# Weight splits, the last turn of the local attention and the latent queries put in another order

## Chip, core and metric

The kernel runs on one NeuronCore of a Trainium2 chip. The metric is the device time of one execution in microseconds, as the median of the runs taken. TensorE (PE) multiplies, VectorE (DVE), ScalarE (ACT) and GpSimd (POOL) work beside it, and SyncE (SP) issues most of the weight loads. The engines are programmed separately and meet only at semaphores, so each works through its own list in order, and whatever waits at the head of a list holds all that is queued behind it.

## What is computed

Three transformer layers run over 256 latent tokens of width 1024 (and 256 context tokens in the first). The first two are a block with modulated norms: layer 0 has a convolution beside a neighbourhood attention ("a0" in the kernel) and a SwiGLU, layer 1 has a window attention and a differential attention ("a1") and a mixture of eight experts. The third layer is this, cut to what matters:

```python
xn = rms_norm_2(h, norm_mix_pre)
proj = xn @ w_in
...
gates = jax.nn.sigmoid(proj[..., IN_A + IN_B:] + b_gate)
g_a, g_b = gates[..., :D_MODEL], gates[..., D_MODEL:]
o_a = mixer_dilated(qkv_a, pos) @ w_o_a
o_b = mixer_mla(q_c, kv_c, k_pe, pos, mla_q_norm, w_uq, mla_kv_norm, w_ukv) @ w_o_b
mix = (g_a * o_a + g_b * o_b) @ w_out
h = h + rms_norm_2(mix, norm_mix_post)
hn = rms_norm_2(h, norm_mlp_pre)
ff = jnp.square(jax.nn.relu(hn @ w_ff1)) @ w_ff2
h = h + rms_norm_2(ff, norm_mlp_post)
```

`mixer_dilated` is an attention of 12 heads in three groups of different stride, whose outputs are weighted by their log-denominators and summed ("a2" in the kernel). `mixer_mla` takes the latent queries to 8 heads of 96 columns, of which 32 are rotated, and the latent keys and values to 8 heads of 64 and 64, and attends over all 256 tokens ("a3").

## The kernel before

Every large product is made from three products at reduced precision. A value x is split in hi (a copy of x in the engine's reduced type, made on ACT) and lo (x minus hi, made on DVE), and `mm3` (lines 889 to 892) adds lo·hi, hi·lo and hi·hi. Weights are split in the same way after their load: a tile of up to 128x2048 lies in one of a few slots, `raw`, `whi` and `wlo`. SP loads it when the tile that used the slot before has been consumed, ACT makes `whi` (line 1468) and DVE makes `wlo` (line 1983).

When ACT and DVE make these splits is set by `feed`, called all over their programs. `feed(event)` makes every split that is due for the tiles in use at that event, and `at["ahead"]` tiles more, as far as their slots allow (`next_tiles`). With `ahead` 2 a split is made two tiles early, with 0 only tiles already in use are made. A split is a single long instruction in the engine's list: what is queued behind it waits for it, and for the load it needs.

PSUM is eight banks; `take(ring, ...)` hands them out in turn from a ring (8 is all banks, 4 is banks 0 to 3), and PE waits there until the holder before has been read out. `Due` and `did` keep the semaphore values, so a wait already implied is not written again.

The places around the change:

- Before attention a0 the keys of layer 0 are turned (`l0_turned`, `head_hi`): for each of four row tiles PE transposes, DVE scales the result into `XQ` (line 2325), ACT makes hi (line 1513) and DVE lo (line 2050). PE's first score of a0 waits for the last lo. The call `feed(("ht", "k", t))` stands ahead of this work, with `ahead` 2 for t = 3.
- A norm of two row tiles: ACT sums the squares (line 1474), DVE makes the mean (`means`, line 2055), POOL takes it to the power -0.5 (`rsqrt`, line 2982), then DVE scales the even tile (line 2062) and ACT the odd one (line 1479). PE transposes both (line 896). In `norm_turned` DVE and ACT read the transposes and split them for the product. `means` of the odd tile is DVE's last step ahead of `norm_turned`, whose first step is a `feed`.
- Attention a2 ends with `finished`: a chain of ten small DVE operations and one ACT exponential, then five of 128x256 (lines 2202 to 2212) that give the last rows, `YA[1]` (mix__281 in the profile). PE turns them (`fin`), ACT makes hi and DVE lo into `OAT`, which is needed only after a3, in the product with w_o_a.
- Then PE makes the latent queries (`uq`, two tiles), keys and values (`ukv`, two tiles). ACT applies the sigmoid to the gates (line 1891), copies the queries out scaled (line 1902), DVE copies keys and values out (lines 2867, 2870) and rotates the queries (`rotate`, lines 2780 to 2787). PE turns queries and keys (`mqt`, eight groups), ACT and DVE copy them out, and a3 starts with scores that need all of them.
- After the product with w_out, `post` adds its norm: two sums, the mean, the power on POOL, then the scaled addition to h; `norm_scale("t", ...)` follows for the next norm. A `feed` stands within `post_scaled`.

In `post` the order on DVE is this (lines 2917 to 2929):

```python
means("pms", (name, t), m, D, ("v", at["chain"]))
post_scaled(name, 1, t, bk, yo, gn)
for half in range(2):
    hs = slice(half * 512, half * 512 + 512)
    for s, n in due(("prs", name, t), ("pyo", name, half, t)):
        e.wait_ge(s, n)
    e.scalar_tensor_tensor(out=h_t[t][:, hs], in0=yo[:, hs], scalar=m, in1=h_t[t][:, hs], op0=ALU.mult,
                           op1=ALU.add).then_inc(*did("post", name, t, half))
```

`("prs", name, t)` is POOL's power, which waits for `means`; `post_scaled` is the `feed` and then bank times gain.

## Time and profile before

| | us |
|---|---|
| median of 3 runs | 1921.24 (1919.27 to 1925.32) |
| the profiled execution | 1925.34, span 1923.5 |
| PE busy in the span | 1751.9 (91%) |
| DVE busy | 1250.8 (65%) |
| ACT busy | 824.2 (43%) |
| POOL busy | 134.6 (7%) |
| mean granted clock of PE | 0.943 |

All times of the trace are microseconds from the span's start. A row of the timeline has the start, the duration, the engine, the line, the operation, the tiles out<-in with their shapes, a count where instructions are merged, and in brackets the idle time before it with what ended it. Where rows of one engine overlap a little, the next instruction had begun while the one before was draining; so the step from start to start is what an instruction costs in a row of them. Names: `ps` is any PSUM bank, `keep__58` the small tile of sums, means and maxima, `in__75` the keys' hi of layer 0, `mix__264` and `mlp__289` the odd row tile of a norm, `mix__242` the latent queries, `whi__66`/`wlo__65` the two parts of a weight tile.

### The profile page before, as it was taken

What the parts mean: (1) busy time and instruction counts of PE and PEld (TensorE: products, weight loads), DVE (VectorE), ACT (ScalarE), POOL (GpSimd) and SP (SyncE); (2) the same over time, 40 slices, a digit from 0 to 9 for tenths busy, and PEclk for the clock granted to TensorE, in tenths of its full rate; (3) what the DMA queues carried; (4) which work ended last, traced back from release to release, by engine and by line L of the source; (5) the groups of instructions that cost most, each with busy time, mean ns of one, the idle gap of its engine ahead of it and who ended that gap; (6) DMA issues with size and microseconds to landing.
All of it is one profiled execution on the core that took longest, in us unless ns stands there. A gap on an engine that the chain in (4) does not pass through costs nothing. (4 is left out here: it accounts for less than half of the span.)

```text
span 1923.5 us, 22047 instructions
## 1 busy us (share of the span) xinstructions
PE 1751.9 (91%) x8958; PEld 1466.7 (76%) x8958; DVE 1250.8 (65%) x1709; ACT 824.2 (43%) x999; POOL 134.6 (7%) x128
## 2 busy tenths in 40 slices
PE   4896999899999987899979999999969998889998
PEld 2774777788788866798768888888859766669986
DVE  5356686368755544675668888888886554566643
ACT  5322232422212213333356667776744434435532
POOL 1130000200110011320100000000120000000000
PEclk9896999999999998899869999999999989999999
DMA  7431332245655431211148898888854511144553
GB/s 294 112 110 66 132 132 89 86 175 218 237 212 180 149 137 66 88 45 56 63 162 300 320 336 328 316 321 317 323 202 159 200 60 39 66 149 171 190 187 126
DMA packets 61437, 332.59 MB, mean 173 GB/s; under 512 B 16836, under 2 KB 17411, under 8 KB 28178
## 3 DMA queue, kind: packets, MB, share of 16 engines
q1 hardware_dynamic: 56080, 321.54, 46.4%
q10 hardware_dynamic: 4354, 6.32, 1.0%
q0 software_dynamic: 896, 3.26, 0.5%
q8 instruction: 74, 1.21, 0.3%
q14 instruction: 33, 0.26, 0.0%
HBM read 329.96 MB, written 1.13 MB: 172 GB/s over the span
## 5 line engine op out<-in xcount | busy, mean ns | idle before, releaser
L1983 DVE TENSOR_TENSOR wlo__65<-raw__64,whi__66 128x2048 fp32r<-128x2048 f32 (+2 forms) x64 | 149.4, 2335 | 95.6 <-ACT whi__66 L1468 95.6
L1983 DVE TENSOR_TENSOR wlo__61<-raw__60,whi__62 128x2048 fp32r<-128x2048 f32 (+2 forms) x65 | 145.1, 2232 | 94.3 <-ACT whi__62 L1468 94.2
L1468 ACT ACTIVATE whi__62<-raw__60 128x2048 fp32r<-128x2048 f32 (+2 forms) x65 | 118.9, 1829 | 115.3 <-DMA raw__60<-in_ffn_w 62.7
L1468 ACT ACTIVATE whi__66<-raw__64 128x2048 fp32r<-128x2048 f32 (+2 forms) x64 | 120.7, 1886 | 102.7 <-DMA raw__64<-in_ffn_w 37.9
L1983 DVE TENSOR_TENSOR wlo__69<-raw__68,whi__70 128x2048 fp32r<-128x2048 f32 (+4 forms) x50 | 106.6, 2133 | 28.3 <-ACT whi__70 L1468 28.2
L2016 DVE SCALAR_TENSOR_TENSOR wsum__71<-raw__68,silu_rows 128x1024 f32<-128x1024 f32 x84 | 100.0, 1220 | 5.4 <-DMA raw__68<-in_ada_w 4.9
L1468 ACT ACTIVATE whi__70<-raw__68 128x2048 fp32r<-128x2048 f32 (+4 forms) x50 | 87.5, 1750 | 13.7 <-DMA raw__68<-in_w_ff 11.6
L2982 POOL TENSOR_TENSOR keep__58<-keep__58,keep__59 128x1 f32<-128x1 f32 (+3 forms) x48 | 49.2, 1027 | 630.9 <-DVE keep__58 L2055 630.9
L2238 DVE TENSOR_REDUCE keep__58<-ps 128x1 f32<-128x256 f32 (+1 forms) x104 | 56.6, 545 | 23.2 <-PE ps L892 16.4
L1983 DVE TENSOR_TENSOR wlo__229<-raw__228,whi__230 128x2048 fp32r<-128x2048 f32 (+1 forms) x24 | 50.7, 2111 | 11.7 <-ACT whi__230 L1468 11.7
L1983 DVE TENSOR_TENSOR wlo__225<-raw__224,whi__226 128x2048 fp32r<-128x2048 f32 (+1 forms) x24 | 52.8, 2200 | 0.0
L890 PE MATMUL ps<-ffn__120,wlo__61 128*128 128x512 f32 (+1 forms) x128 | 46.9, 367 | 4.6 <-DVE ffn__121 L2050 3.3
L1468 ACT ACTIVATE whi__226<-raw__224 128x2048 fp32r<-128x2048 f32 (+1 forms) x24 | 42.5, 1771 | 11.4 <-DMA raw__224<-in_moe_w 11.4
L892 PE MATMUL ps<-ffn__120,whi__62 128*128 128x512 f32 (+1 forms) x128 | 46.4, 362 | 0.0
L891 PE MATMUL ps<-ffn__121,whi__62 128*128 128x512 f32 (+1 forms) x128 | 46.4, 362 | 0.0
L890 PE MATMUL ps<-ffn__120,wlo__132 128*128 128x512 f32 x112 | 43.7, 390 | 0.9 <-issue 0.9
L892 PE MATMUL ps<-ffn__120,whi__133 128*128 128x512 f32 x112 | 43.6, 389 | 0.0
L891 PE MATMUL ps<-ffn__121,whi__133 128*128 128x512 f32 x112 | 43.6, 389 | 0.0
L890 PE MATMUL ps<-ffn__120,wlo__65 128*128 128x512 f32 x112 | 43.6, 389 | 0.0
L891 PE MATMUL ps<-ffn__121,whi__66 128*128 128x512 f32 x112 | 43.6, 389 | 0.0
L892 PE MATMUL ps<-ffn__120,whi__66 128*128 128x512 f32 x112 | 43.6, 389 | 0.0
L2016 DVE SCALAR_TENSOR_TENSOR wsum__138<-raw__135,silu_rows 128x1024 f32<-128x1024 f32 x36 | 43.2, 1221 | 0.5
(1084 smaller groups left out, 5469.4 us busy)
## 6 DMA issues: line engine op xcount, KB each, us to landing
raw__68<-in_ada_w SPq DMA_DIRECT2D x26, 1024.0 KB, 4.9
raw__64<-in_moe_w SPq DMA_DIRECT2D x24, 1024.0 KB, 6.5
raw__60<-in_moe_w SPq DMA_DIRECT2D x24, 1024.0 KB, 6.3
raw__68<-in_moe_w SPq DMA_DIRECT2D x16, 1024.0 KB, 5.6
raw__224<-in_moe_w SPq DMA_DIRECT2D x16, 1024.0 KB, 5.0
raw__228<-in_moe_w SPq DMA_DIRECT2D x16, 1024.0 KB, 6.1
raw__135<-in_ada_w SPq DMA_DIRECT2D x13, 1024.0 KB, 5.2
raw__64<-in_ffn_w SPq DMA_DIRECT2D x11, 1024.0 KB, 5.2
```

The costliest lines, as they stand in the source:

```text
L890: e.matmul(out, ll, rh, start=start, stop=False)
L891: e.matmul(out, lh, rl, start=False, stop=False)
L892: return e.matmul(out, lh, rh, start=False, stop=stop)
L1468: e.activation(t.hi(), t.raw(), ACT.Copy).then_inc(*did("hi", i))
L1983: e.tensor_tensor(t.lo(), t.raw(), t.hi().bitcast(F32), ALU.subtract).then_inc(*did("lo", i))
L2016: m = e.scalar_tensor_tensor(out=junk, in0=slot_raw[t.slot][:, c * 1024:c * 1024 + 1024], scalar=1.0, in1=CB[:, v * D:(v + 1) * D], op0=AL ...
L2238: e.tensor_reduce(neg, b[:, 0:u.total], AX.X, ALU.max).then_inc(*link())
L2982: e.tensor_tensor(x, x, EXPO[:, 0:1].broadcast_to([128, n_]) if n_ > 1 else EXPO[:, 0:1], ALU.pow).then_inc(*did(out, *key))
```

## The change

Five edits, in all engines' programs:

1. In ACT's and DVE's lists ahead of a0, `ahead` is 0 for all four key tiles, and the `feed` with 2 follows the last of them.
2. In the norm "s" (third layer's first) DVE waits for POOL's power of the odd tile before `norm_turned`, and splits one tile ahead instead of two until that is done.
3. The turn of the last rows of a2 and their hi and lo (moved to functions `out_turn`, `out_hi`, `out_lo`) leave `attend` and stand after the four `mqt` groups of the first row tile, on ring 8.
4. Of the latent part: the query turns wait for the query rotation alone, ACT copies each query part out right after its `feed`, without the `feed` of the `ukv` tiles, and DVE rotates the queries ahead of copying keys and values. From there to a3 `ahead` is 0 on both.
5. In the norm after w_out, DVE has `ahead` 0 through both `post` and both `norm_scale`, then feeds with 1.

```diff
@@ scalar_program and vector_program, ahead of a0
         for t in range(4):
-            at["ahead"] = 2 if t == 3 else 0
+            at["ahead"] = 0
             l0_turned("k", t, KT3)
+        at["ahead"] = 2
+        feed(("ht", "k", 3))
         attend("a0", convolved)
@@ vector_program, norm "s"
         norm_scale("s", 0)
         norm_scale("s", 1)
+        for s, n in due(("nrs", "s", 1)):
+            e.wait_ge(s, n)
+        at["ahead"] = 1
         norm_turned("s", 0)
+        at["ahead"] = 2
@@ HEADS, and attend in all three programs
+    HEADS["a2"].late = (1, 1)
+        def out_turn(st, g, ring):
+            y, nc_ = HEADS[st].fin[g][:2]
+            b = take(ring, "fin", st, g)
+            for s, n in state["due"](("fy", st, g)):
+                e.wait_ge(s, n)
+            for c in range(nc_):
+                m = tr(b[:, c * 128:(c + 1) * 128], y[:, c * 128:(c + 1) * 128])
+            m.then_inc(*done("fin", st, g))
...
-                if A.has(j) and A.units[j].last:
...
+                if A.has(j) and A.units[j].last and A.units[j].group != A.late:
+                    out_turn(st, A.units[j].group, A.ring)
...
@@ tensor_program, latent part
-                    for s, n in due(("mrot", t), ("mkr", t), ("mk", t)):
+                    for s, n in due(*([("mrot", t)] if w == "q" else [("mkr", t), ("mk", t)])):
                         e.wait_ge(s, n)
...
+            if t == 0:
+                out_turn("a2", HEADS["a2"].late, "8")
         attend("a3")
@@ scalar_program, latent part
         for hf in range(2):
             for t in range(2):
                 feed(("prod", "uq", hf, t))
-        for hf in range(2):
-            for t in range(2):
-                feed(("prod", "ukv", hf, t))
-        for t in range(2):
-            for hf in range(2):
                 for s, n in due(("prod", "uq", hf, t), ("score", "a2", 23, 0)):
                     e.wait_ge(s, n)
                 m = e.activation(QTMS[t][:, hf * 384:(hf + 1) * 384], bank("uq", hf, t)[:, 0:384], ACT.Copy,
                                  scale=96 ** -0.5)
...
+        at["ahead"] = 0
...
+            if t == 0:
+                out_hi("a2", HEADS["a2"].late)
+        at["ahead"] = 2
         attend("a3")
@@ vector_program, latent part
-        for hf in range(2):
-            for t in range(2):
-                feed(("prod", "ukv", hf, t))
+        at["ahead"] = 0
+        for t in range(2):
...
+            rotate(x4[:, :, 64:80], x4[:, :, 80:96], wide(RMC), wide(RMS), tmp, ("mrot", t), ("mqc", t, 1),
+                   *([("mrot", 0)] if t else [("kper", 1)]))
         for t in range(2):
             k4 = v3(KTMS[t], 8)
...
-        for t in range(2):
...
-            rotate(x4[:, :, 64:80], x4[:, :, 80:96], wide(RMC), wide(RMS), tmp, ("mrot", t), ("mqc", t, 1),
-                   *([("mrot", 0)] if t else [("kper", 1)]))
...
+            if t == 0:
+                out_lo("a2", HEADS["a2"].late)
+        at["ahead"] = 2
         attend("a3")
@@ vector_program, after w_out
-        at["ahead"] = 1
+        at["ahead"] = 0
         post("mix", 0, 8, ("mixo", 1, 0), YOs[0], PG)
         norm_scale("t", 0)
         post("mix", 1, 8, ("mixo", 1, 1), YOs[1], PG)
         norm_scale("t", 1)
+        at["ahead"] = 1
+        feed(("prod", "mixo", 1, 1))
         norm_turned("t", 0)
```

## Rows read from the trace of the kernel before

**Rows 1.** The page: busy time and share of the engines.
```profile
PE 1751.9 (91%) x8958; PEld 1466.7 (76%) x8958; DVE 1250.8 (65%) x1709; ACT 824.2 (43%) x999; POOL 134.6 (7%) x128
```

**Rows 2.** Timeline of ACT, DVE and PE ahead of a0, columns as told above.
```profile
152.60 0.69 DVE L2050 TENSOR_TENSOR in__76<-in__79,in__75 128x512 fp32r<-128x512 f32 x1 [0.69 <-ACT in__75 L1513]
154.40 2.29 DVE L1983 TENSOR_TENSOR wlo__61<-raw__60,whi__62 128x2048 fp32r<-128x2048 f32 x1 [1.11 <-ACT whi__62 L1468]
...
158.84 0.55 PE L890 MATMUL ps<-in__75,in__74 64*128 64x256 f32 x1 [7.82 <-ACT in__75 L1513]
...
161.94 0.69 DVE L2238 TENSOR_REDUCE keep__58<-ps 128x1 f32<-128x512 f32 x1 [3.20 <-PE ps L892]
```

**Rows 3.** Timeline, the next wait of PE in a0 and the load behind it.
```profile
174.81 1.92 ACT L1468 ACTIVATE whi__66<-raw__64 128x2048 fp32r<-128x2048 f32 x1 [11.17 <-DMA raw__64<-in_ev_w_in]
...
180.70 0.58 PE L890 MATMUL ps<-in__75,in__74 64*128 64x256 f32 x1 [3.83 <-ACT in__78 L1529]
```

**Rows 4.** Timeline of the norm "s": DVE, POOL, PE.
```profile
1439.30 2.15 DVE L1983 TENSOR_TENSOR wlo__65<-raw__64,whi__66 128x1920 fp32r<-128x1920 f32 x1
1439.47 2.40 POOL L2982 TENSOR_TENSOR keep__58<-keep__58,keep__59 128x1 f32<-128x1 f32 x1 [0.93 <-DVE keep__58 L2055]
...
1443.10 0.48 PE L896 MATMUL ps<-keep__49,mix__264 128*128 128x128 f32 x1 [3.18 <-ACT mix__264 L1479]
```

**Rows 5.** Timeline of PE from the end of a2 to the keys and values.
```profile
1623.18 0.66 PE L1139 MATMUL ps<-mix__244,mix__279 128*128 128x64 f32 x4
...
1627.93 0.69 PE L896 MATMUL ps<-keep__49,mix__281 128*128 128x128 f32 x2 [4.09 <-DVE mix__281 L2212]
...
1629.55 0.69 PE L890 MATMUL ps<-whi__66,mix__246 128*128 128x384 f32 x1 [0.93 <-DVE mix__273 L2050]
...
1635.46 0.33 PE L890 MATMUL ps<-whi__62,mix__246 128*128 128x384 f32 x1
...
1639.62 0.39 PE L890 MATMUL ps<-whi__259,mix__248 128*128 128x512 f32 x1
```

**Rows 6.** Timeline of ACT and DVE in the latent part.
```profile
1624.47 0.21 ACT L1547 ACTIVATE keep__58<-keep__58 128x12 f32<-128x12 f32 x1 [1.35 <-DVE keep__58 L2181]
...
1629.06 1.28 ACT L1891 ACT_TABLE_LOAD   x1
...
1633.97 1.04 ACT L1468 ACTIVATE whi__259<-raw__257 128x1024 fp32r<-128x1024 f32 x1
...
1643.92 1.61 ACT L1902 ACTIVATE mix__242<-ps 128x384 f32<-128x384 f32 x4
1644.05 1.23 DVE L1983 TENSOR_TENSOR wlo__61<-raw__60,whi__62 128x1024 fp32r<-128x1024 f32 x1 [2.79 <-ACT whi__62 L1468]
...
1645.19 0.42 DVE L2867 COPY mix__243<-ps 128x256 f32<-128x256 f32 x1
...
1647.84 0.28 DVE L2780 TENSOR_TENSOR mix__253<-mix__242,keep__49 128x128 f32<-128x128 f32 x1
```

**Rows 7.** Timeline around the start of a3.
```profile
1649.36 0.83 PE L896 MATMUL ps<-keep__49,mix__242 128*96 128x128 f32 x6 [4.10 <-issue]
...
1655.47 1.97 PE L1113 MATMUL ps<-mix__271,mix__270 96*128 96x256 f32 x8 [0.77 <-ACT mix__271 L1513]
...
1656.18 0.42 DVE L2238 TENSOR_REDUCE keep__58<-ps 128x1 f32<-128x256 f32 x1 [1.20 <-PE ps L1113]
```

**Rows 8.** Timeline of the norm after w_out: DVE, POOL, PE.
```profile
1718.30 2.52 POOL L2982 TENSOR_TENSOR keep__58<-keep__58,keep__59 128x1 f32<-128x1 f32 x1 [99.73 <-DVE keep__58 L2055]
...
1725.27 0.41 PE L896 MATMUL ps<-keep__49,mlp__288 128*128 128x128 f32 x1 [2.72 <-DVE mlp__288 L2062]
...
1728.91 0.55 POOL L2982 TENSOR_TENSOR keep__58<-keep__58,keep__59 128x1 f32<-128x1 f32 x1 [2.90 <-DVE keep__58 L2055]
1730.69 0.47 PE L896 MATMUL ps<-keep__49,mlp__289 128*128 128x128 f32 x1 [5.01 <-ACT mlp__289 L1479]
```

**Rows 9.** Busy time of PE by stretch: stretch, length, busy (instructions), granted clock, DMA.
```profile
1538.00:1554.00 16.00, 16.00 (x34) 0.50 0.00 1
```

More of the change, by code:

```diff
@@ L654, in __init__ @@
             self.slot_of, self.held, self.sums, self.gates, self.ring, self.filled = {}, {}, {}, {}, "5", [16] * 40
-            self.begun, self.turns = 16, {}
+            self.begun, self.turns, self.late = 16, {}, None
             c = 0
@@ L1142, in attend @@
                 j = i - A.lag - 3
-                if A.has(j) and A.units[j].last:
-                    g = A.units[j].group
-                    y, nc_ = A.fin[g][:2]
-                    b = take(A.ring, "fin", st, g)
-                    for s, n in state["due"](("fy", st, g)):
-                        e.wait_ge(s, n)
-                    for c in range(nc_):
-                        m = tr(b[:, c * 128:(c + 1) * 128], y[:, c * 128:(c + 1) * 128])
-                    m.then_inc(*done("fin", st, g))
+                if A.has(j) and A.units[j].last and A.units[j].group != A.late:
+                    out_turn(st, A.units[j].group, A.ring)
                 if i in A.gates:
@@ L1513, in high, with out_hi @@
             e.activation(dst, src, ACT.Copy).then_inc(*did(name, *key))
+        def out_hi(st, g):
+            _, nc_, dst, t0 = HEADS[st].fin[g]
+            feed(("fin", st, g))
+            high("fhi", (st, g), dst[0][:, 0:nc_, t0:t0 + 128], v3(bank("fin", st, g)[:, 0:nc_ * 128], nc_),
+                 ("fin", st, g), *HEADS[st].out_free)
         def attend(st, fill=None):
@@ L1559, in attend @@
                 j = i - A.lag - 3
-                if A.has(j) and A.units[j].last:
-                    g = A.units[j].group
-                    _, nc_, dst, t0 = A.fin[g]
-                    feed(("fin", st, g))
-                    high("fhi", (st, g), dst[0][:, 0:nc_, t0:t0 + 128], v3(bank("fin", st, g)[:, 0:nc_ * 128], nc_),
-                         ("fin", st, g), *A.out_free)
+                if A.has(j) and A.units[j].last and A.units[j].group != A.late:
+                    out_hi(st, A.units[j].group)
         e.dma_start(cst, cst_d[:, 0:NCORE]).then_inc(*did("cst", by=16))
@@ L2214, in finished, with out_lo @@
                 empties(("o", st, (t, 1)), ("fy", st, g))
+        def out_lo(st, g):
+            _, nc_, dst, t0 = HEADS[st].fin[g]
+            feed(("fin", st, g))
+            low("flo", (st, g), dst[1][:, 0:nc_, t0:t0 + 128], v3(bank("fin", st, g)[:, 0:nc_ * 128], nc_),
+                dst[0][:, 0:nc_, t0:t0 + 128], ("fhi", st, g))
+            empties(("fin", st, g), ("flo", st, g))
         def attend(st, fill=None, between=None):
@@ L2277, in attend @@
                 j = i - A.lag - 3
-                if A.has(j) and A.units[j].last:
-                    g = A.units[j].group
-                    _, nc_, dst, t0 = A.fin[g]
-                    feed(("fin", st, g))
-                    low("flo", (st, g), dst[1][:, 0:nc_, t0:t0 + 128], v3(bank("fin", st, g)[:, 0:nc_ * 128], nc_),
-                        dst[0][:, 0:nc_, t0:t0 + 128], ("fhi", st, g))
-                    empties(("fin", st, g), ("flo", st, g))
+                if A.has(j) and A.units[j].last and A.units[j].group != A.late:
+                    out_lo(st, A.units[j].group)
                 if i in A.gates:
@@ L2378, in vector_program @@
         for t in range(4):
-            at["ahead"] = 2 if t == 3 else 0
+            at["ahead"] = 0
             l0_turned("k", t, KT3)
+        at["ahead"] = 2
+        feed(("ht", "k", 3))
         attend("a0", convolved)
@@ L2885, in vector_program @@
                 empties(("mqt", w, t, 0), ("mq_v", w, t, 0))
+            if t == 0:
+                out_lo("a2", HEADS["a2"].late)
+        at["ahead"] = 2
         attend("a3")
@@ L2931, in vector_program @@
             post_scaled("mix", 0, t, ("mixo", 0, t), YOs[t], PG, ("bg",))
-        at["ahead"] = 1
+        at["ahead"] = 0
         post("mix", 0, 8, ("mixo", 1, 0), YOs[0], PG)
```

6 lines of the change are left out of this document (3 added, 3 removed).

## Prediction

> **What bounds the kernel now.** I read the page's busy shares first [rows 1]: TensorE (PE) is busy for 91% of the span, DVE for 65%, ACT for 43%. So only PE's idle time can be won, some 170 us, and only where PE waits for another engine that itself does something that can wait. Then I read the waits of PE, longest first, and for each the timeline of DVE, ACT and POOL just before it. Five of the longest stand at the five edits: 7.82 us ahead of a0, with 3.83 us behind it [rows 2, 3], 3.18 us in the norm "s" [rows 4], 4.09 and 0.93 us at the end of a2 [rows 5], 4.10 us at the query turns [rows 7] and 5.01 us in the norm after w_out [rows 8]. What the reader is to see in each is which instruction of DVE stands in the chain that PE waits for without belonging to it. Last I read PE's granted clock by stretch: it is 1.00 or 0.50 (2.4 or 1.2 GHz), and falls in several of these waits.
>
> **1. Keys of layer 0.** The last key tile's scaling can follow the lo of the third, which starts at 152.60 and lasts 0.69 [rows 2]; it stands behind wlo__61, which waits for its hi and runs 154.40 to 156.69. From that end to PE's first score at 158.84 are 2.15 us of scaling, hi, lo. Starting at 153.3 instead, PE goes at 153.3 + 2.15 = 155.4, which is 3.4 us sooner. The split isn't gone: ACT makes its hi right after the keys' hi, which ends some 0.8 us ahead of PE's start (the lo of 0.69 follows it), at 154.6; that hi takes 1.9 as a like one [rows 3], until 156.5, and wlo__61 takes 2.29, until 158.8. PE reads it after the first score, which lasts 161.94 - 158.84 = 3.1 with its wait, so at 158.5: it is late by 0.3. Score 0's maximum on DVE stood at 161.94 and now stands at 158.8, 3.2 us sooner. The next wait of PE ends at 180.70 and comes from a load that ACT waited 11.17 us for [rows 3]. That load was issued on a release by DVE, whose sums follow the maximum of 161.94, so it moves along and the wait keeps its length. Taken: 3.2 us. Bounds: 0 if that load's landing doesn't move, 3.4 if all does.
>
> **2. Norm "s".** POOL's power takes 0.55 us [rows 8], but 2.40 when it comes up 0.17 us after the start of a weight split on DVE, and it ends 0.42 after that split [rows 4]. The added wait holds DVE's list until POOL is done: POOL 1439.47 to 1440.02, ACT scales the odd tile, PE turns at 1443.10 - 1.85 = 1441.25. Behind the waiting DVE stand wlo__65 (2.15) and the first read of the transposes. The split now runs 1440.1 to 1442.25, the first four transposes end at about 1442.2, so nothing is late; a second split in that place would be, which `ahead` 1 avoids. It goes behind the norm, and PE reads it after the first tile's products. Gain 1.85 us. Bounds 0 to 1.85.
>
> **3 and 4. From a2 to a3.** I write the new timeline out, since the two edits share it. PE ends a2's last product at 1623.18 + 0.66 = 1623.8 [rows 5] and waits for the ten small and five larger DVE steps of `finished`, then once more for the lo of the turned rows (the bank is reused): 1629.55. Without the turn there it goes on at 1623.8 with `uq`, whose weights are split and whose banks 0 to 3 were read. PE doesn't idle, so I take full clock: half of `uq` takes 1639.62 - 1635.46 = 4.16 us [rows 5], all of it 8.3: 1632.1. `ukv` took from 1639.62 to DVE's first copy of it at 1645.19 [rows 6], so 5.5: PE is through at 1637.6.
> ACT loses the moved hi ahead of the sigmoids. Its last small exponential of a2 ends at 1624.7 [rows 6]; table load and two sigmoids took 1633.97 - 1629.06 = 4.9 us [rows 6], now until 1629.6. Then come the two hi of `ukv` at about 1.0 and four query copies at 0.40 [rows 6], interleaved: 3.6 us, until 1633.2. DVE's two lo (1.23 each [rows 6], a little less from start to start) follow the hi: 1630.7 to 1631.9, and 1632.4 to 1633.6. PE wants the first at 1632.1. Next the two rotations: the step from the first rotation's start to PE's turn is 1649.36 - 1647.84 = 1.52 [rows 6, 7], two are 3.0: 1636.6. Then eight copies of keys and values in 1647.84 - 1645.19 = 2.65 us: 1639.2.
> PE needs only the first rotation (1635.1) for the query turns, so it starts them at 1637.6 as soon as `ukv` is done: 4.10 us of waiting go. Eight groups of four (0.45 each at full clock, an estimate from the six in 0.83 [rows 7]) and the two moved transposes (0.3) end at 1641.5, with the keys' and DVE's copies just ahead of each. ACT's last copy ends at 1642.1, and a3's first scores start at 1642.2 instead of 1655.47 [rows 7]: 13.2 us sooner.
> But not all of this stays. The two splits of w_o_a used to lie in DVE's and ACT's idle time of the latent part (the second at 1644.05, after 2.79 us of idling [rows 6]); with `ahead` 0 they now stand in a3, ahead of the first maximum. ACT: 1642.1 + 2 x 1.0 = 1644.1, DVE: first lo at 1643.1, second to 1645.4. The maximum that stood at 1656.18 [rows 7] comes at 1645.4: 10.8 us sooner, not 13.2. ACT's exponential table load (1.28, the duration is that of [rows 6]) lies beside DVE's second split. From there a3 runs as before, since its steps are paced by the chain maximum, exponential, turn, and what it feeds later is the same. The moved hi and lo cost ACT and DVE nothing: between their mqt copies they wait for PE. Gain 10.8 us. Bounds: 6.1 (only the 4.09 + 0.93 wait and its slow clock, less the splits: 5.7 + 2.8 - 2.4) and 13.2.
>
> **5. Norm after w_out.** POOL's power of the first `post` took 2.52 us beside wlo__65 [rows 8]. With `ahead` 0 it takes 0.55, so the first half of h is ready 2.0 us sooner. The second `post` stood behind the scaling of the even tile, so at 1725.1 (PE's 1725.27 waits for that scaling). Now it waits for ACT's square of PE's last bank, which PE leaves at 1725.27 - 2.72 = 1722.55; with 0.8 for the square, an estimate, that is 1723.4, so 1.7 us sooner. Yet the split hasn't vanished: it now comes right behind `means` of the odd tile, without a wait for POOL such as edit 2 has. POOL's power of that tile, 0.55 at 1728.91 [rows 8], then comes up beside it as in [rows 4] and takes about 2.5: 2.0 lost. PE's turn, at 1730.69, stands 0.3 later. Bounds: 1.7 gained (POOL gets in first), 0.3 lost; I take the loss, since the two stretched powers of POOL in the trace both stand there, right behind a mean with a split behind it. The Trainium skill ("SBUF — State Buffer", Who interferes with whom) says that a VectorE tensor_tensor with both inputs in SBUF and a GpSimd instruction reading SBUF exclude each other, and that the one issued first decides; it speaks against this edit. By that rule PE's turn is 0.3 late, and without it 1.7 early.
>
> **Sum.** 3.2 + 1.85 + 10.8 - 0.3 = 15.6 us. On the profiled execution 1925.34 - 15.6 = 1909.7; that execution lies 4.1 above the median of 1921.24, and the three runs spread over 6 us, so for a median I take 1921.24 - 15.6 = 1905.6. The rest of the kernel is a chain of releases by PE and moves along.
>
> **Rivals.**
> *The clock falls at a3's start.* PE's four scores take 1.97 [rows 7] and end at 1644.2, and the first turn, 1.27 us behind the first maximum as in the rows before, waits until about 1646.7: a new gap of 2.5 us, where there was none. In a2 the clock stood at 0.50 for 16 us after a gap [rows 9]; after the 4.09 of [rows 5] the first half of `uq` took 1635.46 - 1629.55 = 5.9 us instead of 4.16. So the price is 1.75 us for a short fall, and at most half of 16 for one as long as in a2; a3 has slack on PE, so I take up to 5. Result 1907 to 1910.5. The Trainium skill ("TensorE: Matmul & The Clock Gate", Part 1) has the half rate follow an idle stretch; by it this gap is a candidate, and whether it suffices no row shows.
> *Part of the latent gain comes back.* If ACT is late with its copies, or a bank in ring 8 is read later than I have it, a3 starts with the bound of 6.1 instead of 10.8: 1910.3. For it speaks that DVE and ACT have no slack from 1629.6 on; against it that PE is at `ukv` until 1637.6 in any case.
> *Edit 5 wins.* Then 2.0 less: 1903.6.
> *The edits hit nothing.* If the splits kept their place and load landings set the pace, only edit 2 is left: 1919.4. The bracket of DMA in [rows 3] speaks for it in one place; the load's issue behind DVE's sum against.
> *Slower.* Place: a0 and a2, in whose 64-row products the clock stayed at 0.50 once it had fallen [rows 9]. At half clock PE does 1 us of work in 2. The shift moves each fall; to eat 15.6 us and 5.8 more, the low stretches must grow by 43 us, nearly three times the one of [rows 9]. Result above 1927.
>
> **How the numbers follow.** A difference under 0.3% (5.8 us) can't be told from none here. Forecast 1905.6 as it stands 0.55; clock in a3 0.17; part comes back 0.11; edit 5 wins 0.08; hits nothing 0.06; slower 0.03. The range reaches from 1900 (edit 5 wins and a low stretch of the clock is spared) to 1913 (both losses in the latent part together, or half of edit 1 lost beside one). Faster by over 0.3%, below 1915.5: 0.91; within 0.06; slower 0.03.
>
> **What would show it.** Right: PE's wait ahead of a0 at 4.4 us; POOL's second power in the norm "s" at 0.55; no wait at the end of a2 and none at the query turns; a3's first maximum some 2.4 us late behind two lo splits of 128x1024; POOL's odd power after w_out at 2.5 with a split beside it. Wrong: a3's first scores more than 20 us behind the start of `uq`; a wait of 180.70's kind grown by what edit 1 won; a POOL power of 0.55 in that last place.

## The result, and the profile after

The changed kernel takes 1906.47 us (median of 4 runs, 1904.22 to 1909.57) beside 1923.28 us of the kernel before in the same session (4 runs, 1919.27 to 1925.96): a ratio of 0.9919, 95% interval 0.9904 to 0.9933. The profiled execution took 1909.57 us with a span of 1907.7, against 1925.34 and 1923.5 before.

The engines' busy times and TensorE's granted clock from the page of the changed kernel (the clock in tenths of full speed, 40 slices). TensorE's busy time is that of before [rows 1], so by the whole span what was won is idle time:

```profile
PE 1751.4 (92%) x8958; PEld 1468.4 (77%) x8958; DVE 1250.2 (66%) x1709; ACT 824.2 (43%) x999; POOL 132.6 (7%) x128
...
PEclk9897999999999998999869999999998999799999
```

The timeline of TensorE in the changed kernel, those instructions that answer to the waits of before (start, duration, engine, line, operation, in brackets the idle time before it and who ended it):

```profile
156.12 0.55 PE L891 MATMUL ps<-in__75,in__74 64*128 64x256 f32 x1 [4.42 <-ACT in__75 L1518]
...
159.53 0.77 PE L891 MATMUL ps<-in__86,wlo__61 128*128 128x512 f32 x1 [0.34 <-issue]
...
178.14 0.58 PE L891 MATMUL ps<-in__75,in__74 64*128 64x256 f32 x1 [3.65 <-ACT in__78 L1540]
...
1438.93 0.48 PE L897 MATMUL ps<-keep__49,mix__264 128*128 128x128 f32 x1 [1.34 <-ACT mix__264 L1484]
...
1611.13 0.42 PE L891 MATMUL ps<-whi__66,mix__246 128*128 128x384 f32 x1
...
1625.11 1.04 PE L897 MATMUL ps<-keep__49,mix__242 128*96 128x128 f32 x8
...
1629.72 1.97 PE L1123 MATMUL ps<-mix__271,mix__270 96*128 96x256 f32 x8 [0.73 <-ACT mix__271 L1518]
...
1634.22 0.62 PE L897 MATMUL ps<-keep__49,mix__274 128*128 128x128 f32 x2 [2.54 <-ACT mix__274 L1540]
...
1715.38 0.47 PE L897 MATMUL ps<-keep__49,mlp__289 128*128 128x128 f32 x1 [7.41 <-ACT mlp__289 L1484]
...
1719.40 0.55 PE L891 MATMUL ps<-mlp__286,wlo__65 128*128 128x256 f32 x1 [0.56 <-DVE mlp__287 L2058]
```

The rows at 156.12, 178.14 and 1438.93 answer to 7.82 and 3.83 us [rows 2, 3] and 3.18 us [rows 4]; at 159.53 the first product that reads the moved split wlo__61 is late by 0.34 us. At 1611.13 the query products start with no wait at all, where 4.09 and 0.93 us stood [rows 5], and the wait of 4.10 us at the query turns [rows 7] is gone as well (1625.11). The wait of 2.54 us at 1634.22, just after a3's first scores, is new.

The timelines of VectorE and GpSimd in the changed kernel, around four of its moved weight splits:

```profile
1437.14 0.55 POOL L3001 TENSOR_TENSOR keep__58<-keep__58,keep__59 128x1 f32<-128x1 f32 x1 [0.93 <-DVE keep__58 L2063]
...
1437.73 2.16 DVE L1991 TENSOR_TENSOR wlo__65<-raw__64,whi__66 128x1920 fp32r<-128x1920 f32 x1 [0.66 <-POOL keep__58 L3001]
...
1630.59 1.23 DVE L1991 TENSOR_TENSOR wlo__65<-raw__64,whi__66 128x1024 fp32r<-128x1024 f32 x1 [1.02 <-ACT whi__66 L1473]
1631.74 1.22 DVE L1991 TENSOR_TENSOR wlo__61<-raw__60,whi__62 128x1024 fp32r<-128x1024 f32 x1
1632.87 0.42 DVE L2253 TENSOR_REDUCE keep__58<-ps 128x1 f32<-128x256 f32 x1
...
1711.46 2.28 DVE L1991 TENSOR_TENSOR wlo__65<-raw__64,whi__66 128x2048 fp32r<-128x2048 f32 x1
...
1711.62 2.52 POOL L3001 TENSOR_TENSOR keep__58<-keep__58,keep__59 128x1 f32<-128x1 f32 x1 [2.90 <-DVE keep__58 L2063]
```

GpSimd's power of the local norm takes 0.55 us instead of 2.40 [rows 4], and the split waits for it. Both splits of w_o_a stand ahead of a3's first maximum (1632.87). In the last norm the odd tile's power now lies beside a split and takes 2.52, as the prediction had it.

What remains is TensorE's granted clock. Stretches of the changed kernel (length, TensorE's busy time, granted clock, DMA share, GB/s); the last row answers to the next fence:

```profile
1534.00:1564.00 30.00, 30.00 (x131) 0.98 0.20 70
1634.00:1658.00 24.00, 23.78 (x91) 0.51 0.00 1
...
1432.00:1452.00 20.00, 12.95 (x66) 0.74 0.53 182
```

The kernel before, the 20 us that start at the same point of its local norm:

```profile
1434.00:1454.00 20.00, 10.79 (x42) 0.57 0.41 146
```

a2's start, at 0.50 before [rows 9], is nearly all at full clock now; a3, which had full clock, runs for 24 us at 0.51, the lower of the two levels (1.2 GHz); and behind the norm "s" the clock is back sooner.

Between marks on TensorE's timeline (each the start of the instruction named) the two traces stand like this:

| from, to | before | after | change |
|---|---|---|---|
| start of the span, a0's first score | 158.84 | 156.12 | -2.72 |
| to a1's first score | 650.35 | 650.63 | +0.28 |
| to the router's first product | 164.73 | 164.77 | +0.04 |
| to the odd tile's first transpose, norm "s" | 469.18 | 467.41 | -1.77 |
| to a2's first score | 94.52 | 92.47 | -2.05 |
| to the first query product | 91.93 | 79.73 | -12.20 |
| to a3's first score | 25.92 | 18.59 | -7.33 |
| to a3's first turn | 1.98 | 4.50 | +2.52 |
| to w_o_a's first product | 22.62 | 30.31 | +7.69 |
| to the odd tile's first transpose, norm "t" | 50.62 | 50.85 | +0.23 |
| to the first MLP product | 4.92 | 4.02 | -0.90 |
| to the last product | 181.84 | 182.18 | +0.34 |

They add up to -15.87 us. The experiments ask which of these rows are the edits' and which are the clock's. One row needs care although its change is small: from a0's first score to a1's it takes 641.1 to 650.6 us in the 14 traces of this case, and both of these executions lie at its long end. The kernel before ran beside each group of them, with medians of 1920.68, 1922.66, 1921.72 and 1921.98 us; single runs of one kernel lie up to 16 us apart, so for terms of 2 us the traces decide and not the medians.

### The profile page after: what moved, and what is told of

Read it like the earlier page. It is cut to its first block and busy times, and to the rows that moved or that the text cites. A ratio compares the mean times of both kernels' runs of the same rounds, so it can differ in the third digit from the quotient of the medians.

```text
span 1907.7 us, 22049 instructions
## 1 busy us (share of the span) xinstructions
PE 1751.4 (92%) x8958; PEld 1468.4 (77%) x8958; DVE 1250.2 (66%) x1709; ACT 824.2 (43%) x999; POOL 132.6 (7%) x128
## 5 line engine op out<-in xcount | busy, mean ns | idle before, releaser
L1473 ACT ACTIVATE whi__70<-raw__68 128x2048 fp32r<-128x2048 f32 (+4 forms) x50 | 87.5, 1750 | 13.7 <-DMA raw__68<-in_w_ff 11.6
```

The source lines that it names most:

```text
L1473: e.activation(t.hi(), t.raw(), ACT.Copy).then_inc(*did("hi", i))
```

## The experiments

**The latent part alone: edits 3 and 4 on the kernel before.** Edits 1, 2 and 5 are undone, for instance:

```
-        for s, n in due(("nrs", "s", 1)):
-            e.wait_ge(s, n)
-        at["ahead"] = 1
         norm_turned("s", 0)
-        at["ahead"] = 2
```

> Edits 3 and 4 alone on the kernel before. Theory A (the chain): 10.8 us under before if a3 runs at full clock; the profile of the changed kernel has a3 at a granted clock of 0.50 for 23 us, which cost 7.8 us there, so 3 us under before if that low stretch belongs to the new gap of 2.5 us at a3's start, and the low stretch of 16 us at a2's start stays. Theory B (the low stretches fall by chance, whatever the edits): a3's clock is at 1.00 in about half of the runs, and a2's low stretch is long or short without regard to the edits.

Measured: 1911.68 us, ratio 0.996 (0.994 to 0.998). From the first query product to a3's first score it takes 18.58 us, and the new wait is there, yet a3 takes 23.50 instead of 30.31 us. Its trace, two stretches of a3 right behind that wait:

```profile
1644.00:1648.00 4.00, 4.00 (x19) 0.58 0.00 0
1648.00:1667.00 19.00, 15.53 (x107) 1.00 0.01 1
```

By the medians it is 9.0 us under the kernel before, so neither theory's number: the chain of theory A is there, but a3's low stretch is not the one of the changed kernel. The wait of 2.54 us brought the clock down here too, but for some 3 us and not for 24. In a2 it kept the low stretch of before (17 us), and a2 to the first query product took 86.01. So with the same low stretch in a2 and a3 left out, the edits bring 91.93 - 86.01 = 5.9 us there, 25.92 - 18.58 = 7.3 behind it, less 4.50 - 1.98 = 2.5: 10.7 us. The 7.3 hold 1.7 us of clock, since the wait of before, 4.09 us, slowed the query products behind it (10.07 us there, 8.43 in the changed kernel).

**The rest alone: edits 1, 2 and 5 on the kernel before.** The latent part keeps the old order; the diff is the part of the change that the last experiment left out.

> Edits 1, 2 and 5 without 3 and 4. Theory A: 3.2 + 1.85 - 0.3 = 4.8 us under before, and, if edit 2 is what shortened the low stretches of the clock in the norm and at a2's start, 8 us more, so 13; a3 at full clock. Theory B: 4.8 us, with a2's low stretch long or short by chance.

Measured: 1912.98 us, ratio 0.9964 (0.9951 to 0.9976). It is 7.7 us under the kernel before by the medians, between the 4.8 and 13 of theory A. a0's first score stands at 155.91, the odd tile's first transpose in the norm "s" 467.43 us behind the router's first product, and from there to a2 it is 92.51: edit 2 brings 2.0 us behind the norm beside the 1.8 in it. a3 (22.61 us) and the stretch at its start (1.98) are those of before. a2 keeps its low stretch of 17 us (91.64 us to the query products), so edit 2 is not what shortened it in the changed kernel's trace.

**One edit: the keys' split (edit 1).**

```
         for t in range(4):
-            at["ahead"] = 2 if t == 3 else 0
+            at["ahead"] = 0
             head_hi("k", t, KT3)
+        at["ahead"] = 2
+        feed(("ht", "k", 3))
```

> The kernel before with edit 1 alone: one weight split of the two engines is turned behind the last keys' split, the rest is as before. Theory A (the chain): TensorE's idle time ahead of a0's first score is 4.42 us instead of 7.82, the waits that follow it stay, stages from a1 on are as long as in the kernel before to 0.3 us wherever the granted clock is the same, and the median is 3.2 us below the kernel before (ratio 0.998), with +-5 us from the clock in the light attention stages. Theory B (the 11 us that the edits of the latent stage showed do not depend on the rest, but edit 1 brings nothing of its own because the wait in a0 comes back behind it): the idle time at 180.7 grows from 3.8 to about 7 us and the median is that of before. Either way the stretch between the last second-layer... product of a2 and a3's first score stays at 25.9 us, since edits 3 and 4 are left out.

Measured: 1916.51 us, ratio 0.9976 (0.9958 to 0.9995). The interval allows for the 3.2 us and for more than twice as much, so the trace decides, and it says theory A. TensorE ahead of a0:

```profile
155.74 0.55 PE L890 MATMUL ps<-in__75,in__74 64*128 64x256 f32 x1 [4.42 <-ACT in__75 L1513]
```

The next wait, at 177.76, is 3.63 us and hasn't grown. Nothing that was won is given back.

**Edit 2 without its wait.**

```
         norm_scale("s", 1)
-        for s, n in due(("nrs", "s", 1)):
-            e.wait_ge(s, n)
         at["ahead"] = 1
```

> The changed kernel without the one wait of VectorE for GpSimd's power ahead of the split in the local stage's norm; the split keeps its new place behind the norm's scales. It asks whether the place or the wait brought edit 2's 1.8 us. Theory A (the wait brings it: without it split and power run side by side again): the power near 1437 takes 2.4 us instead of 0.55, TensorE's gap ahead of the second tile's transposes is 3.2 us instead of 1.3, and the stretch to the first transposed norm is 469.2 us instead of 467.4. Theory B (the place brings it): 0.55 us and 467.4 stay, without the 0.66 us that VectorE waits.

Measured: 1908.07 us, ratio to before 0.9934 (0.9912 to 0.9955). GpSimd, VectorE and TensorE in its norm "s", and the granted clock there:

```profile
1434.06 2.40 POOL L2999 TENSOR_TENSOR keep__58<-keep__58,keep__59 128x1 f32<-128x1 f32 x1 [0.93 <-DVE keep__58 L2063]
...
1433.90 2.15 DVE L1991 TENSOR_TENSOR wlo__65<-raw__64,whi__66 128x1920 fp32r<-128x1920 f32 x1
...
1437.69 0.47 PE L897 MATMUL ps<-keep__49,mix__264 128*128 128x128 f32 x1 [3.18 <-ACT mix__264 L1484]
...
1430.00:1450.00 20.00, 12.20 (x50) 0.58 0.44 147
```

Power, wait and stage (469.17 us) are those of the kernel before: the wait brings the gain, and the new place of the split alone nothing (theory A). The Trainium skill ("SBUF — State Buffer", Who interferes with whom) has it that a VectorE instruction with two inputs in SBUF and a GpSimd one that reads SBUF contend; the 2.40 against 0.55 us agrees. It shows a second gain too, which no step of the prediction had. The stretch from this norm to a2 is 94.71 us, against 92.47 with the wait. It holds over all traces without work ahead of a2: 94.4 to 94.7 us in the four kernels whose wait here is 3.18 us (before, edits 3 and 4 alone, edit 1 alone, this one), 92.4 to 92.7 in six of the seven with 1.33 or 1.34, and 93.7 in the seventh (work in a3's wait). What lies between is the clock: it is low for 17 us behind the longer wait, for 10 in the six and for 14 in the seventh (0.58 or 0.57 against 0.74 in 20 us).

**The same wait in the norm after w_out.** The changed kernel with two lines more:

```
         norm_scale("t", 1)
+        for s, n in due(("nrs", "t", 1)):
+            e.wait_ge(s, n)
         at["ahead"] = 1
```

> The changed kernel with one wait more: VectorE waits for GpSimd's power of the odd tile of the last norm before its weight split of the MLP stage, as the change does it in the norm of the local stage. Theory A (VectorE's split, which reads two operands from SBUF, stretches GpSimd's operation beside it): that power takes 0.55 us instead of 2.52, TensorE's wait of 7.41 us ahead of the transposes near 1715 falls by 1.7 to 2.0 us less what the split now starts later (up to 0.6), and the stretch from the output product to the first transposed norm is 49 to 49.7 us instead of 50.85; ratio to the changed kernel 0.999. Theory B (GpSimd's operation is long for another reason, its two instruction kinds or its place behind the first): it stays near 2.5 us, the split starts that much later and the stage is 1 to 2 us longer.

Measured: 1906.30 us, ratio to before 0.9912 (0.9885 to 0.9938), so the median doesn't tell it from the changed kernel. The trace does: GpSimd and TensorE in the last norm, then a2's and a3's starts.

```profile
1713.81 0.55 POOL L3003 TENSOR_TENSOR keep__58<-keep__58,keep__59 128x1 f32<-128x1 f32 x1 [2.90 <-DVE keep__58 L2063]
...
1715.60 0.48 PE L897 MATMUL ps<-keep__49,mlp__289 128*128 128x128 f32 x1 [5.44 <-ACT mlp__289 L1484]
...
1526.00:1546.00 20.00, 18.40 (x41) 0.57 0.15 52
1636.00:1660.00 24.00, 23.50 (x89) 0.51 0.00 1
```

The stage takes 48.80 us instead of 50.85, so the wait is worth 2.05 us: theory A, and the explanation of edit 5's loss holds. Over all traces it is 48.8 to 49.0 us in the three with this wait, and 50.7 to 50.9 in six of the seven that have edit 5 without it (53.15 in the seventh, the changed kernel's second trace, with the clock low at the start of the stage). In a2, up to which this kernel and the changed one are the same, the clock is low for 17 us again, which takes back 85.82 - 79.73 = 6.1 us.

**The order without the late turn (edit 4 alone in the latent part).** The changed kernel, with the last rows of a2 turned where they were:

```
-    HEADS["a2"].late = (1, 1)
...
-            if t == 0:
-                out_turn("a2", HEADS["a2"].late, "8")
```

> The changed kernel with the last rows of a2 turned where the kernel before turned them (inside a2's last steps); the new order of the latent stage (queries scaled and rotated ahead of keys and values, no weight split in between) stays. It says which of the edits 3 and 4 the 10.6 us come from. Theory A (the order carries most): TensorE's wait of 4.1 us at a2's end for the rows' finish comes back, ahead of the query products, but the engines are then free later by no more than 1 us, so from a2's last product to a3's first score it is 18.6 plus 4 to 5 us, and the median is 4 to 5 us above the changed kernel (about 1910 to 1912). Theory B (the late turn carries most): the stage takes over 27 us of the 30 that it took before and the median is 8 us or more above the changed kernel. Theory C (the late turn costs what it saves, since it now lies between the queries' transposes): 18.6 us or less and no difference.

Measured: 1916.09 us, ratio 0.9973 (0.9955 to 0.9991). TensorE at a2's end and a3's start:

```profile
1613.41 0.69 PE L896 MATMUL ps<-keep__49,mix__281 128*128 128x128 f32 x2 [4.09 <-DVE mix__281 L2215]
...
1615.04 0.69 PE L890 MATMUL ps<-whi__66,mix__246 128*128 128x384 f32 x1 [0.93 <-DVE mix__273 L2053]
...
1635.06 1.97 PE L1122 MATMUL ps<-mix__271,mix__270 96*128 96x256 f32 x8 [0.78 <-ACT mix__271 L1515]
...
1639.43 0.69 PE L896 MATMUL ps<-keep__49,mix__274 128*128 128x128 f32 x2 [2.40 <-ACT mix__274 L1537]
...
1638.00:1656.00 18.00, 16.57 (x62) 0.53 0.00 1
```

The wait is back, and from a2's last product to a3's first score it is 1635.06 - (1613.41 - 4.09) = 25.7 us, between theory A (22.6 to 23.6) and B (27), while the median lies 8 us or more above the changed kernel, as B had it: the wait costs its 5.0 us and, since the clock falls in it, another 1.7 in the query products, which take 10.1 instead of 8.4. Before, the same stretch took 31.6 [rows 5, 7]. So the order is worth 5.9 us and the late turn 7.1 more. The medians differ by more (9.6 us from the changed kernel's first, 11.6 from its second); 0.9 of it are told below, and what the clock took elsewhere in these runs isn't known. The wait in a3's start (2.40) comes with the order, since that is what leaves both splits to a3.
The stretch from norm "t" to the first MLP product tells one thing more: it is 4.9 us in the five kernels without the late turn (among them this one, with 4.91) and 4.0 in all with it. TensorE's first MLP product waits 1.46 us there, for an ACT operation that reads the norm's transposed rows, and 0.56 for VectorE's split in the changed kernel. The late turn takes its bank from the ring of eight and not from the ring of four that the MLP uses as well, so that the MLP starts one bank further back; that this frees the first product is read from the two releasers, and no run changed it alone.

**a3's splits spread out.** The changed kernel with no weight split at a3's start, and one each from its steps 4 and 10 on:

```
             for i in A.steps():
+                if st == "a3":
+                    at["ahead"] = 0 if i < 4 else 1 if i < 10 else 2
```

> The changed kernel, with the two weight splits of w_o_a made in a3's step 4 and 10 instead of ahead of its first maximum. Theory A: the gap of 2.54 us at a3's start goes, so a3 begins 2.4 us sooner, its clock stays at 1.00 and the 7.8 us of the low stretch come back: 8 to 10 us under the changed kernel, less 1 or 2 for the splits within a3. Theory C (the splits only move the wait): each split of 1.2 us delays a3's chain by its length, and nothing is won but the clock.

Measured: 1912.14 us, ratio 0.9948 (0.9925 to 0.9971). The wait at the start is gone (2.07 us from first score to first turn), and a3 takes 31.83 us, longer than in the changed kernel. ACT and TensorE at a3's fourth step, and the clock behind it:

```profile
1637.18 1.05 ACT L1473 ACTIVATE whi__66<-raw__64 128x1024 fp32r<-128x1024 f32 x1
...
1640.93 0.66 PE L1149 MATMUL ps<-mix__244,mix__279 128*128 128x64 f32 x4 [2.50 <-ACT mix__279 L1550]
...
1642.00:1662.00 20.00, 19.79 (x76) 0.50 0.00 1
```

The split that ACT and VectorE do at this step holds up a copy that TensorE needs. The wait hasn't gone; it has moved, with nearly its size, and the clock falls behind it for 20 us. That is theory C, without the clock that it hoped to win.

**Work in a3's wait.** The changed kernel; TensorE runs two constant products (128x128 by 128x512, never read) after the fourth score of a3; the trace counts each as two:

```
+                if (st, i) in SPINS:
+                    spin("o", SPINS[st, i])
```

> The changed kernel, with two matmuls of 128x128 by 128x512 of constants put in PE's gap ahead of a3's first turn, into a bank that nobody reads; they are added work and feed nothing. Theory A (idle time of PE lets the clock fall, and a3's light load keeps it low): clock 1.00 through a3 and 7.8 us under the changed kernel, though PE does more. Theory B (chance, or a3's load alone): the clock falls as before, and the time is the same or 1 us longer.

Measured: 1900.64 us, ratio 0.9895 (0.9878 to 0.9911). TensorE at a3's start, and the clock of all a3:

```profile
1630.04 1.88 PE L1113 MATMUL ps<-keep__49 128*128 128x512 f32 x4
...
1632.74 0.41 PE L899 MATMUL ps<-keep__49,mix__274 128*128 128x128 f32 x2 [0.82 <-ACT mix__274 L1551]
...
1633.00:1655.00 22.00, 18.36 (x125) 1.00 0.00 1
```

The first turn stands as far behind the first score as without them (4.50 us), so the chain isn't any shorter; only the clock is another, and a3 takes 22.55 us instead of 30.31: theory A. The medians differ by less (5.8 us from the changed kernel's first, 3.9 from its second), and in this trace a2 had a low stretch of 14 us. A single step shows why. Two scores of a3 that follow each other, first in the changed kernel, then two pairs in this one:

```profile
1640.93 1.17 PE L1123 MATMUL ps<-mix__271,mix__270 96*128 96x256 f32 x2
...
1643.06 1.17 PE L1123 MATMUL ps<-mix__271,mix__270 96*128 96x256 f32 x2
```

```profile
1635.83 0.65 PE L1132 MATMUL ps<-mix__271,mix__270 96*128 96x256 f32 x2
...
1636.93 0.65 PE L1132 MATMUL ps<-mix__271,mix__270 96*128 96x256 f32 x2
...
1638.55 0.65 PE L1132 MATMUL ps<-mix__271,mix__270 96*128 96x256 f32 x2
```

At the lower clock a step takes 2.13 us, all of it TensorE's work; at full clock 1.10 and 1.62 in turn, 1.36 on average, set by the other engines.

**The changed kernel once more.** Nothing is edited.

> The changed kernel once more, unchanged. What is asked is whether the long stretch at the lower clock in a3 (23.9 us in its first profile, 3.3 us in the kernel with edits 3 and 4 alone, which has the same wait of 2.5 us) belongs to this kernel or to the execution. Theory A (it belongs to the execution): all waits of the chain come back to 0.1 us (4.42, 3.65, 1.34, 2.54, 7.41), and a3 takes either 23.5 or about 30 us, whichever; the same of a2's low stretch of 3.3 or 17 us. Theory B (it belongs to the kernel): a3 takes 30.3 us and a2's stretch is 79.7 us again. Median 1904 to 1909 either way.

Measured: 1904.52 us, ratio 0.9927 (0.9905 to 0.9949). a2's and a3's starts:

```profile
1524.00:1544.00 20.00, 19.92 (x76) 0.91 0.15 57
1626.00:1650.00 24.00, 22.95 (x87) 0.51 0.00 1
```

a2 took 79.89 us and a3 30.40, like the first trace: theory B, by these two. (In a2 the clock fell twice here, for some 3 us each time, at 1524 and 1575.) But more traces bear on it. Three other kernels have the same code up to a2's end (a3's splits spread out, work in a3's wait, the added wait in norm "t"), and in these a2 has a low stretch of 17, 14 and 17 us. So a2's part changes between executions of the same code, and theory A holds for it. a3 is at 30.3 us or more in all three traces with the same code up to there, so its part may belong to the kernel.

**Work in four waits, and the kernel before with the same.** Constant products ahead of a0's first score, behind a0's first turn, ahead of a2's first score and in a3's start, with norm "t"'s added wait; in the kernel before, the first three.

```
+    SPINS = {('a3', 3): 2}
+    AHEAD = {"a0": 2, "a2": 3}
...
+            if st in AHEAD:
+                spin(A.ring, AHEAD[st])
...
+                if st == "a0" and i == 3:
+                    spin("o", 3)
```

> The changed kernel, with VectorE's wait for GpSimd's power in the last norm as well, and with constant matrix products (128x128 by 128x512, results overwritten unread) that TensorE runs in four of its waits: two ahead of a0's first score (wait 4.42 us), three behind a0's first turn (3.65), three ahead of a2's first score (3.3), two in a3's start (2.54). Each is meant to end before what TensorE waits for is there. Theory A (the lower clock in the light attention stages starts in these waits, and work in them keeps it up): a2 shows no low stretch or one of 3 us, a3 none, a0's second one of 17 or so is 7 or less; a2's last product comes 6 to 12 us sooner and the median is 1889 to 1896 us, 10 or more below the changed kernel. Theory B (it falls from what comes behind the waits, for each of these stages is light on TensorE): a3 gains as the earlier filler showed (some 6 us on average), a0 and a2 nothing, and the median is 1898 to 1902.

> The kernel before with the same constant products in its own three waits (ahead of a0's first score, behind a0's first turn, ahead of a2's first score); a3 has no such wait there. It asks what the four edits are worth once the clock is treated alike. Theory A (edits and clock are separate terms): it is below the kernel before by what the fillers win in a0 and a2 (4 to 12 us), and above the filled changed kernel by the chain's terms: 3.2, 1.8, 10.6 and 2 us for the added wait, together some 17 us. Theory B (the edits' gain was in part a better clock): the distance between the two filled kernels is under 13 us.

Measured: 1898.29 us, ratio 0.9885 (0.9868 to 0.9901), and 1920.02 us, ratio 0.9995 (0.9983 to 1.0007). Neither is what theory A had. TensorE ahead of a2 in the filled changed kernel:

```profile
1522.11 4.54 PE L1114 MATMUL ps<-keep__49 128*128 128x512 f32 x6 [3.41 <-DVE mix__252 L2837]
1526.58 0.70 PE L1135 MATMUL ps<-mix__243,mix__242 64*128 64x256 f32 x2
```

The constant products didn't run in the wait but after it: their bank was that of the first score, still being read. The stretch ahead of a2 takes 97.09 us instead of 92.47. That was my error, not the chip's. Behind it a2 takes 78.24 us, with the clock up, so even so it is 3 us ahead of a trace with the low stretch (92.50 + 85.82 against 97.09 + 78.24).
The distance of the two filled kernels is 21.7 us by the medians, over the 17 of theory A and far from theory B: the edits' gain isn't a better clock by chance. Edit 2's clock behind norm "s" (98.92 against 97.09 us, 1.8) and the MLP's bank (0.9) make 2.7 of the 4.7 us above 17.

**The same with a free bank.** One edit on the last:

```
-    AHEAD = {"a0": 2, "a2": 3}
+    AHEAD = {"a0": ("4", 3), "a2": ("o", 3)}
```

> The filled changed kernel once more, with the three products ahead of a2 put into an accumulator bank that is free during the wait. In the last run they were written to the bank of a2's first score, which the two copies of the last latent rows still held: they waited 3.4 us for that, and a2's first score came 4.6 us later than without them. Ahead of a0 there are now three products instead of two. Theory A (the fillers' cost was this wait alone): the stretch from the local norm's second transposes to a2's first score is 92.5 us again instead of 97.1, a2 to its query products stays at 78 to 80 us, and the median is 3 to 5 us below the last one: 1893 to 1896, ratio to the kernel before 0.986. Theory B (a2's clock stayed up only because the fillers ran right up to its first score): 92.5 us as well, but a2 takes 84 to 86 us and the median is 1898 to 1900 as before.

Measured: 1893.62 us (1891.92 to 1895.31), ratio 0.9853 (0.9837 to 0.9869), theory A. TensorE ahead of a2, then the clock of a2 and of a3:

```profile
1523.09 2.74 PE L1114 MATMUL ps<-keep__49 128*128 128x512 f32 x6
1526.44 0.48 PE L1135 MATMUL ps<-mix__243,mix__242 64*128 64x256 f32 x1 [0.61 <-DVE mix__252 L2837]
...
1532.00:1604.00 72.00, 70.23 (x328) 1.00 0.20 66
1624.00:1650.00 26.00, 21.55 (x135) 1.00 0.00 1
```

92.37 us to a2, 78.21 in it, 22.54 in a3, and no low stretch in either. This is the best version of the case: 11 to 13 us below the changed kernel, of which 2 are the wait in norm "t".

## Why the prediction was right, and where its size was luck

**Edit 1.** Predicted: TensorE's wait at 4.4 us, the net 3.2. Measured 4.42, in the trace of edit 1 alone as well. The start of that wait stands 0.68 us later in the changed kernel's trace (156.12 - 4.42 against 158.84 - 7.82), so a0's first score came 3.4 sooner, and the next wait, 3.65, didn't grow. The moved split was late by 0.34 us where 0.3 was forecast, which leaves some 3.1. Right.

**Edit 2.** Predicted 1.85, measured 1.77 in the stage, by the mechanism named. Too small all the same: behind a wait of 1.3 us and not 3.2 the clock rose sooner, worth 2.05 us more. The clock had been counted among the risks and nowhere among the gains.

**Edits 3 and 4.** Predicted 10.8 to a3's first maximum. With like clock in a2: 5.9 or 6.0 (91.93 - 86.01 or - 85.96), 7.3 and -2.5, so 10.7 or 10.8. The single steps hold too: query products 8.43 us (8.3), keys and values 5.55 (5.5), turns to first score 4.61 (4.6), the maximum 3.15 us behind the first score (3.2). The late turn gave another 0.9 us at the MLP's first product by the banks' rotation, which wasn't seen; the argument had followed the moved turn on every engine's list, but not in the ring of banks.

**Edit 5.** Predicted +0.3, measured +0.23, by both halves of the argument: GpSimd's first power in this stage takes 0.55 us instead of 2.52, and counted from w_o_a's first product the odd tile's power comes up at 47.09 us instead of 48.84, 1.75 sooner (1.7 forecast); then it takes 2.52 us as said. That the loss is the split beside it is shown by the wait that takes it away (-2.05).

**The rival that came true: the clock at a3's start.** Its cause was right (a new wait of 2.5 us; measured 2.54) and its price wasn't. I took 1.75 to 5 us on the ground that TensorE has slack in a3, and gave it a chance of 0.17. It costs 7.7: at 0.51 TensorE is busy for 23.78 of 24 us, so the slack is gone and it becomes the bound, with steps of 2.13 us instead of 1.36. Nine such steps follow each other, at 0.77 us more each: 7 of the 7.7 us. A clock fall was seen in all seven traces with a wait of 2.4 to 2.54 us in a3 (the one that moved to the fourth step is among them), and in none of the seven where no wait was longer than 1.1 us. The chance should have been far over one half. The price could have been read in a3 of before: TensorE is busy for 17.33 of the 20 us from 1658 on, and work that fills nearly nine tenths of a stage at full clock can't fit into it at half.

**Why the number fitted.** The sum of the edits was 15.6 us. The traces give 18.5 us for them: 3.2 + 1.8 + 10.8 - 0.2, and 2.05 + 0.9 that were missed. The clock took 7.7 us in a3. In a2 it gave back 6.2 in this trace (79.73 against 85.96 at like order), for no reason of the change that the runs show: of five traces of the same code two are low for only 3 or 7 us there, the others for 14 to 17. That makes 17.0, and the other 1.1 lie in rows of the table that no edit touches and in the start of a0's wait, 0.68 us later. So the profiled execution came out at 1909.57 where the sum had 1909.7, by what was missed on either side: 2.9 us of gain and the clock's 6.2 against its 7.7 and this 1.1. Had a2 kept its low stretch, it would have been some 1916 us, outside the range. For the median, 1906.5 against 1905.6, not even this is shown: the profiled execution is the slowest of the four, the other three left no trace, and the stretch from a0's first score to a1's alone differs by up to 9.6 us between traces. That it came within 1 us is luck as well.

**Open.** How long the lower clock lasts once it has fallen. In a3, behind the same wait of 2.54 us, it was 24 us in three traces and some 3 in two (the two kernels without edit 2's wait), and 17 behind the 2.40 of another; no experiment changed this alone. I can't say whether that belongs to the kernel or only looks so.
Behind a0's first turn the lower clock came back in the best version too (at 178, for some 14 us), with constant products in most of that wait; they ended 2.44 us ahead of the score there.

## What to carry to other kernels

When a step is moved away from a wait, look what the wait becomes at its new place. If it is as long as those of a3 here (2.4 us), price it with TensorE at the lower clock for the whole stage behind it: if TensorE is busy for well over half of that stage at full clock, it becomes the bound there, and a step costs its work at half clock. From what length on such a wait costs, no run shows. Where such a wait can't be taken away, constant products in it cost nothing that these traces show (18.57 to 18.59 us to a3's first score, 4.50 or 4.51 to its first turn, with and without) if they end before the awaited data is there and go to a bank that is free at that time: check the bank, since otherwise they wait themselves and come on top. And read the waits behind a wait that gets shorter: the clock's earlier return was half of what edit 2 gave.

## What the runs showed of the hardware

**In a3 a wait of 2.4 to 2.54 us brought the clock down each time, and it then stayed down for a varying time.** A wait of that length doesn't do so everywhere: the changed kernel's wait of 2.64 us at 775.65 passed with the clock at 1.00 from 768 to 790. And in the changed kernel's second trace the clock fell twice for some 3 us behind waits of 0.81 and 1.02 us (granted clock 0.57 in 1575 to 1579 and in 1657 to 1661). So the length of the wait alone doesn't tell. a3's cost by what stood at its start (first turn to w_o_a's first product):

| wait of 2.4 to 2.54 us | at the lower clock | a3 | traces |
|---|---|---|---|
| none (no wait over 1.1 us) | 0 | 22.5 to 22.6 us | 7 |
| at the start | some 3 us | 23.5 us | 2 |
| at the start | 17 us | 28.5 us | 1 |
| at the start | 24 us | 30.3 to 30.4 us | 3 |
| at the fourth step | 20 us | 31.8 us | 1 |

a2, in kernels with the late turn, takes 78.2 us where constant products fill most of the wait ahead of it; behind waits of 3.1 to 3.5 us it takes 79.7 to 79.9 with 3 or 7 us at the lower clock, 84.2 with 14, and 85.8 to 86.0 with 17. The Trainium skill ("TensorE: Matmul & The Clock Gate", Part 1) says that the point at which the clock changes differs between runs of one kernel. It tells this of the rise behind a kernel's start; the five traces of a2 with the same code show a like difference behind a fall, 3 to 17 us.

**A short GpSimd operation that comes up beside a VectorE subtraction of two SBUF tiles ends only behind it.** 0.55 us became 2.40 and 2.52, ending 0.4 us behind the subtraction in the local norm (1433.90 + 2.15 against 1434.06 + 2.40), and one wait of VectorE undid it in both places: 1.8 and 2.05 us, at a cost that no later stage shows.
